# Squares and fourth weight split to GpSimd, factors from the bank, and filler products, in three seams of a two-block transformer kernel

## The chip, the cores and the metric

One Trainium2 chip, one core. The metric is the device time of a whole execution in microseconds, median of several. TensorE multiplies, VectorE, ScalarE and GpSimd work elementwise, SyncE issues most DMAs. Each engine runs its instructions in order; between engines they wait on counting semaphores.

## The reference, cut to what matters

Two transformer blocks over a stream of 512 tokens by 1024 channels, in fp32. The second block is the one touched:

```python
h = x
h = h + 0.5 * rms_norm(swiglu(rms_norm(h, ffn1_pre_g), ...), ffn1_post_g)
u = rms_norm(h, mix_pre_g);  proj = u @ w_in;  ...           # sparse attention, gated recurrence
h = h + rms_norm(merged @ w_out, mix_post_g)
h = h + 0.5 * rms_norm(swiglu(rms_norm(h, ffn2_pre_g), ...), ffn2_post_g)
ple_gate = sigmoid(rms_norm(h, ple_pre_g) @ w_ple_gate)
h = h + rms_norm(ple_gate * (p @ w_ple_proj), ple_post_g)
```

where `rms_norm(x, g) = x * rsqrt(mean(x * x) + eps) * g`.

## The kernel before

The stream lies transposed in SBUF as `x`, eight chunks (k = 0 to 7) of 128 channels by 512 tokens. Weights come as units of 128 by 1024 (or 1408) from HBM into four slots `raw`. To multiply in fp32 with fast passes, every operand is split into a high part (`w_hi`, `a_hi`: a rounded copy, made by ScalarE) and a low part (`w_lo`, `a_lo`: operand minus high part), and each product is three matmuls: hi by hi, lo by hi, hi by lo. `unit_high_part` is ScalarE's half of a weight unit, `split_unit` the other half, on VectorE (L1957, one instruction of 1024 columns) or on GpSimd (L715, four pieces of 256 columns). Units are split in one order, and `unit_split` counts them; a unit's slot is free again when `unit_done` says that TensorE is through with it.

A *seam* is the place where a branch ends, is normed, added to the stream, and the next norm begins. There are three in the second block: behind the first feed-forward (`post1`, then `mixpre` for the stage `proj2`), behind the mixer (`postmix`, then `pre2` for `up3`), and behind the second feed-forward (`post2`, then `plepre` for `ple`). The branch lies kept in `y`. For `post1` and `postmix`, `total_x` on TensorE sums the squares over channels (`sum_columns`, L839, one column of ones) and, when ScalarE has the root and VectorE its inverse, spreads the factor by four transposes over the bank `stat_bank` (`spread`, L872). For `post2` these two lie between products of the small stage `pproj`. Then comes the loop `add_branch` on VectorE, for each chunk k:

- `chunk = y[k] * g[k] * factor` (L2054); the factor is read from the bank for k = 0 and from its copy `rstd` (L1917) afterwards;
- `x[k] += chunk` (L2056);
- the square of chunk k - 1 is added to `sum_sq` (`add_square`: copy L1994, adds L1997), for the next norm;
- `a_lo[k] = x[k] * g'[k] - a_hi[k]` (`scaled_low`, L1963), which waits for ScalarE;
- at some k a weight split: at k = 4 the fourth unit (`first + 3`) of the next stage in the first two seams, at k = 0 and 2 units of `ple` in the third.

ScalarE's side is `scaled_highs` (for `ple` a loop of its own): `a_hi[k] = x[k] * g'[k]` (L1394) when x[k] is there, the square of x[k] into one of two buffers `sq` (L1372), and behind k = 3 the high part of the fourth unit. A square waits until the one two before it is added.

TensorE runs `first_three` (L897 to L899): for each k, as soon as a_lo[k] is there, that chunk's nine matmuls of the stage's first three tiles, since the norm's factor can be applied to the product afterwards. For `mixpre` and `pre2` three more belong to the fourth tile from k = 5 on; for `plepre` the third tile runs two chunks late. Then TensorE sums the squares, does the rest of the fourth tile (L823 to L825) and spreads the factor.

GpSimd does nothing in the seams: ahead of the first it waits for `unit_split` to reach the fourth unit of `proj2`, to split the fifth and later ones; behind its last differences for the recurrence it ends.

Of the kernel before, what the change touches and what calls it, by code (L numbers as in the profile page):

```python
# [38 lines left out]
P = 128  # L39
# [302 lines left out]
def two_blocks(nc, ins, spill, bias_rows, out):  # L342

    with ExitStack() as ctx:
# [362 lines left out]
        def _(pool):  # L707
# [21 lines left out]

            def split_for(t):  # L730

                u = UNIT["proj2"][0] + t + 3
                split_unit(u, BLOCKS_OF[u] * P)
# [18 lines left out]
            pool.wait_ge(unit_split, UNIT["proj2"][0] + SLOTS)  # L752
# [21 lines left out]
            for n in range(HEADS * (NEAR - 1)):  # L774
                make_diff(n)


        @block.tensor
        def _(pe):
# [100 lines left out]
            def total_x(name):  # L880
                sum_x(name)
                spread(name)

# [206 lines left out]
            total_x("post1")  # L1090
# [193 lines left out]
            total_x("postmix")  # L1284
# [44 lines left out]
        def _(act):  # L1329
# [66 lines left out]
            def scaled_highs(stage, g, before, units):  # L1396

                for k in range(DC):
# [3 lines left out]
                    if k == 3:  # L1402
# [491 lines left out]
        def _(dve):  # L1894
# [71 lines left out]
            def scaled_done(stage, units):  # L1966
# [5 lines left out]
                if units.startswith("up"):  # L1972
                    split_unit(UNIT[units][0] + 4)
# [69 lines left out]
            def add_branch(name, g, src, last_read, signal, before, split=None, units={}):  # L2043
# [3 lines left out]
                for k in range(DC + 1):  # L2047
                    if k < DC:
                        if last_read is not None:
                            wait(last_read(k))  # L2050
                        if k >= 2:
                            dve.wait_ge(signal, before + k - 1)
                        factor = rstd if k else stat_bank
                        step(v.scalar_tensor_tensor(chunk[:, k % 2, :], src[:, k, :], prm(g, k), factor[:, :],  # L2054
                                                    ALU.mult, ALU.mult))
                        v.tensor_tensor(x[:, k, :], x[:, k, :], chunk[:, k % 2, :], ALU.add).then_inc(signal, 1)  # L2056
                    if k == 0:
                        take_rstd(name)
                    if k and split:
                        add_square(split[0], k - 1)  # L2060
                    if k < DC and split:
                        scaled_low(split[0], split[1], k)
# [282 lines left out]
            def branch_kept(stage, square_stage):  # L2345
                for k in range(DC):
# [3 lines left out]
                    if k < DC - 1 or square_stage not in LAST_ON_PE:  # L2350
# [6 lines left out]
                       split=("mixpre", "mix_pre_g"), units={4: UNIT["proj2"][0] + 3})  # L2357
# [252 lines left out]
            for m in range(DC):  # L2610
# [13 lines left out]
                if m + 1 < DC:  # L2624
# [6 lines left out]
                       split=("pre2", "ffn2_pre_g"), units={4: UNIT["up3"][0] + 3})  # L2631
            scaled_done("pre2", "up3")
            hiddens("up3", 2)
            for c in range(2):
# [8 lines left out]
                       split=("plepre", "ple_pre_g"), units={0: UNIT["ple"][0] + 1, 2: UNIT["ple"][0] + 2})  # L2643
# [129 lines left out]
```

## Time and profile before

| | us |
|---|---|
| median of 3 runs | 1894.69 |
| lowest and highest | 1892.78, 1895.48 |
| profiled execution | 1894.94 |
| its span, first to last instruction | 1892.8 |

Granted TensorE clock over the span: 0.992 of full speed. Matmuls overlap, so a matmul row shows a longer duration than the distance to the next one. A time in square brackets at the end of a row of the order of time is the idle time of that engine ahead of the instruction, and what ended it.

### The profile page before, as it was taken

How to read it: one execution, taken by the hardware profiler on the slowest of the kernel's cores; microseconds unless marked ns; L12 is line 12 of the kernel's file. 1: busy time of each engine (PE TensorE's matmuls, PEld its weight loads, DVE VectorE, ACT ScalarE, POOL GpSimd, SP SyncE). 2: the span in 40 equal slices, each digit the busy share in tenths (PEclk: the TensorE clock that was granted, in tenths of full speed). 3: DMA queues.
4: the chain of work that ended last, by engine and by line, in shares of the span. 5: the costliest groups of instructions: out<-in, count | busy, mean ns of one | idle time of the engine just before them, and what ended most of it. 6: DMA issues, size and time to landing. Idle time of an engine off the chain costs nothing.

```text
span 1892.8 us, 23659 instructions
## 1 busy us (share of the span) xinstructions
PE 1821.3 (96%) x8356; PEld 1469.0 (78%) x8356; DVE 1089.7 (58%) x1658; ACT 665.9 (35%) x1010; POOL 207.6 (11%) x272
## 2 busy tenths in 40 slices
PE   6998999999999999999989998999898999999988
PEld 4676888888888888888866776789776888888866
DVE  6565588888334655542262677587666655552265
ACT  5333333333223222222243334565453322232244
POOL 2332000000000000000024454433000000000000
PEclk9999999999999999999999999999999999999999
DMA  4677232323222222232222233232341323233211
GB/s 157 61 84 45 89 111 100 100 90 117 94 87 89 89 100 100 90 117 92 83 87 69 95 126 134 73 108 77 117 143 57 102 98 100 92 119 106 83 61 73
DMA packets 55459, 180.61 MB, mean 95 GB/s; under 512 B 6336, under 2 KB 7104, under 8 KB 55392
## 3 DMA queue, kind: packets, MB, share of 16 engines
q1 hardware_dynamic: 43344, 157.33, 24.8%
q10 hardware_dynamic: 12048, 22.40, 7.6%
q8 instruction: 40, 0.66, 0.1%
q14 instruction: 27, 0.22, 0.0%
HBM read 167.65 MB, written 12.06 MB: 95 GB/s over the span
## 4 chain that ended last, share of the span: by engine, by line
PE 82%; DVE 10%; ACT 3%; DMA 2%; issue 2%; ACTq 0%; POOL 0%; SPq 0%; DVEq 0%
PE bank L801 20%; PE bank L802 20%; PE bank L803 20%; PE bank L823 3%; PE bank L825 2%; PE bank L824 2%; DVE score L2399 2%; PE bank L897 2%; PE bank L898 1%; PE bank L899 1%; DVE best L2398 1%; DMA raw<-in_w_proj 1%; PE bank L839 1%; PE bank L1148 1%; PE bank L1232 1%
## 5 line engine op out<-in xcount | busy, mean ns | idle before, releaser
L1341 ACT ACTIVATE w_hi<-raw 128x1024 fp32r<-128x1024 f32 (+2 forms) x281 | 305.0, 1089 | 737.1 <-PE bank L803 625.4
L801 PE MATMUL bank<-a_hi,w_hi 128*128 128x512 f32 x1192 | 467.0, 392 | 3.1 <-DVE gate L2383 2.1
L803 PE MATMUL bank<-a_hi,w_lo 128*128 128x512 f32 x1192 | 464.7, 390 | 0.0
L802 PE MATMUL bank<-a_lo,w_hi 128*128 128x512 f32 x1192 | 464.5, 390 | 0.0
L1957 DVE TENSOR_TENSOR w_lo<-raw,w_hi 128x1024 fp32r<-128x1024 f32 (+2 forms) x222 | 284.2, 1280 | 255.3 <-ACT w_hi L1341 242.0
L801 PEld LDWEIGHTS bank<-a_hi,w_hi 128*128 128x128 f32 x1192 | 224.2, 188 | 57.9 <-issue 7.7
L715 POOL TENSOR_TENSOR w_lo<-raw,w_hi 128x256 fp32r<-128x256 f32 x196 | 150.1, 798 | 1018.0 <-ACT w_hi L1341 1018.0
L803 PEld LDWEIGHTS bank<-a_hi,w_lo 128*128 128x128 f32 x1192 | 224.1, 188 | 47.4
L802 PEld LDWEIGHTS bank<-a_lo,w_hi 128*128 128x128 f32 x1192 | 224.1, 188 | 45.7
L801 PE MATMUL bank<-h_hi,w_hi 128*128 128x512 f32 x528 | 205.4, 389 | 0.0
L802 PE MATMUL bank<-h_lo,w_hi 128*128 128x512 f32 x528 | 205.4, 389 | 0.0
L803 PE MATMUL bank<-h_hi,w_lo 128*128 128x512 f32 x528 | 205.4, 389 | 0.0
L802 PEld LDWEIGHTS bank<-h_lo,w_hi 128*128 128x128 f32 x528 | 99.1, 188 | 20.7
L803 PEld LDWEIGHTS bank<-h_hi,w_lo 128*128 128x128 f32 x528 | 99.1, 188 | 20.6
L801 PEld LDWEIGHTS bank<-h_hi,w_hi 128*128 128x128 f32 x528 | 99.1, 188 | 20.4
L823 PE MATMUL bank<-a_hi,w_hi 128*128 128x512 f32 x250 | 108.0, 432 | 0.0
L825 PE MATMUL bank<-a_hi,w_lo 128*128 128x512 f32 x250 | 99.0, 396 | 0.0
L824 PE MATMUL bank<-a_lo,w_hi 128*128 128x512 f32 x250 | 98.7, 395 | 0.0
L2316 DVE TENSOR_TENSOR val<-bank,rstd 128x512 f32<-128x512 f32 x44 | 30.4, 691 | 113.6 <-PE bank L803 113.6
L897 PE MATMUL bank<-a_hi,w_hi 128*128 128x512 f32 x150 | 63.9, 426 | 31.3 <-DVE a_lo L1963 29.9
L897 PEld LDWEIGHTS bank<-a_hi,w_hi 128*128 128x128 f32 x150 | 29.8, 199 | 45.2 <-DVE a_lo L1963 29.7
L898 PE MATMUL bank<-a_lo,w_hi 128*128 128x512 f32 x150 | 61.2, 408 | 0.0
(330 smaller groups left out, 2315.5 us busy)
## 6 DMA issues: line engine op xcount, KB each, us to landing
raw<-in_w_up SPq DMA_DIRECT2D x132, 512.0 KB, 3.4
raw<-in_w_down SPq DMA_DIRECT2D x48, 704.0 KB, 4.0
raw<-in_w_proj SPq DMA_DIRECT2D x59, 512.0 KB, 3.5
raw<-in_w_wo SPq DMA_DIRECT2D x8, 512.0 KB, 3.6
raw<-in_w_branch SPq DMA_DIRECT2D x16, 256.0 KB, 2.7
gates_in<-spill ACTq DMA_DIRECT2D x16, 256.0 KB, 2.9
raw<-in_w_out SPq DMA_DIRECT2D x8, 512.0 KB, 3.9
raw<-in_w_ple SPq DMA_DIRECT2D x8, 512.0 KB, 3.4
```

The source lines that it names most:

```text
L715: made = pool.tensor_tensor(lo[:, part], src[:, part], hi[:, part].bitcast(F32), ALU.subtract)
L801: mm(dst[:, :], wh, hi[:, k, :], start=(first and c == 0), stop=False)
L802: mm(dst[:, :], wh, lo[:, k, :], start=False, stop=False)
L803: step = mm(dst[:, :], wl, hi[:, k, :], start=False, stop=(last and c == n - 1))
L823: mm(dst[:, :], wh, a_hi[:, c, :], start=(c == 0), stop=False)
L824: mm(dst[:, :], wh, a_lo[:, c, :], start=False, stop=False)
L825: step = mm(dst[:, :], wl, a_hi[:, c, :], start=False, stop=(c == DC - 1))
L897: mm(dst[:, :], wh, hi[:, k, :], start=(k == 0), stop=False)
L898: mm(dst[:, :], wh, lo[:, k, :], start=False, stop=False)
L1341: fn(w_hi[:, slot, 0:size], raw[:, slot, 0:size], ACT.Copy).then_inc(unit_high, 1)
L1957: v.tensor_tensor(w_lo[:, slot, 0:size], raw[:, slot, 0:size], w_hi[:, slot, 0:size].bitcast(F32), ALU.subtract).then_inc(unit_split, 1)
L2399: step(v.match_replace(score[i][:, :], best[:, :], score[i][:, :], TAKEN))
```

## The change

Four edits, all about the three seams.

1. *Squares on GpSimd.* `add_square` leaves the loop of VectorE. GpSimd gets `add_squares`: when the former norm's inverse is there, it copies the first square and adds the other seven, in all three seams. As an operation on GpSimd the add is one instruction of 512 columns.
2. *Fourth split on GpSimd.* For `proj2` and `up3` the fourth unit is split by GpSimd between the squares 2 and 3; ScalarE makes its high part behind k = 2 instead of k = 3. VectorE waits for it ahead of the fifth unit of an `up` stage. In the third seam VectorE keeps its two splits.
3. *Factors from the bank.* The copy to `rstd` is gone, and all eight chunks read the factor from `stat_bank`. The count that frees the bank rises at the last chunk.
4. *Small products.* `total_x` waits for a tile to be read and, behind `spread`, issues twelve products of `ident` and `ones`, 128 by 128 by 128 in plain fp32, into the first auxiliary bank. Nobody reads them. This is in the first two seams.

```diff
+            def add_squares(stage, former, fourth=None):
+
+                pool.wait_ge(inverse_ready, SUM[former] + 1)
+                for k in range(DC):
+                    q = square_at(stage, k)
+                    pool.wait_ge(sq_ready, q + 1)
+                    if k == 0:
+                        pool.tensor_copy(sum_sq[:, :], sq[:, q % 2, :]).then_inc(sum_added, 1)
+                    else:
+                        pool.wait_ge(sum_added, q)
+                        pool.tensor_tensor(sum_sq[:, :], sum_sq[:, :], sq[:, q % 2, :], ALU.add).then_inc(sum_added, 1)
+                    if fourth and k == 2:
+                        pool.wait_ge(unit_split, UNIT[fourth][0] + 3)
+                        split_unit(UNIT[fourth][0] + 3, DC * P)
+
...
             split_units("wo", 0, SLOTS)
-            pool.wait_ge(unit_split, UNIT["proj2"][0] + SLOTS)
+            add_squares("mixpre", "post1", "proj2")
             split_units("proj2", SLOTS, LEAD2 + 3)
...
                 make_diff(n)
+            add_squares("pre2", "postmix", "up3")
+            add_squares("plepre", "post2")
...
-            def total_x(name):
+            def total_x(name, idle):
+
+                wait(tile_read(idle, 0))
                 sum_x(name)
                 spread(name)
+                for _ in range(12):
+                    mm(bank[BANKS][:, 0:P], ident[:, :], ones[:, :], start=True, stop=True)
...
-            total_x("post1")
+            total_x("post1", "up2")
...
-            total_x("postmix")
+            total_x("postmix", "out")
...
-                    if k == 3:
+                    if k == 2:
                         unit_high_part(UNIT[units][0] + 3)
...
                 if units.startswith("up"):
+                    dve.wait_ge(unit_split, UNIT[units][0] + SLOTS)
                     split_unit(UNIT[units][0] + 4)
...
-            def add_branch(name, g, src, last_read, signal, before, split=None, units={}):
+            def add_branch(name, g, src, last_read, signal, before, split, units={}):
 
                 invert(name)
                 dve.wait_ge(spread_ready, STAT[name] + 1)
-                for k in range(DC + 1):
-                    if k < DC:
-                        if last_read is not None:
-                            wait(last_read(k))
-                        if k >= 2:
-                            dve.wait_ge(signal, before + k - 1)
-                        factor = rstd if k else stat_bank
-                        step(v.scalar_tensor_tensor(chunk[:, k % 2, :], src[:, k, :], prm(g, k), factor[:, :],
-                                                    ALU.mult, ALU.mult))
-                        v.tensor_tensor(x[:, k, :], x[:, k, :], chunk[:, k % 2, :], ALU.add).then_inc(signal, 1)
-                    if k == 0:
-                        take_rstd(name)
-                    if k and split:
-                        add_square(split[0], k - 1)
-                    if k < DC and split:
-                        scaled_low(split[0], split[1], k)
+                for k in range(DC):
+                    wait(last_read(k))
+                    if k >= 2:
+                        dve.wait_ge(signal, before + k - 1)
+                    step(v.scalar_tensor_tensor(chunk[:, k % 2, :], src[:, k, :], prm(g, k), stat_bank[:, :],
+                                                ALU.mult, ALU.mult))
+                    if k == DC - 1:
+                        dve.sem_inc(rstd_ready, 1)
+                    v.tensor_tensor(x[:, k, :], x[:, k, :], chunk[:, k % 2, :], ALU.add).then_inc(signal, 1)
+                    scaled_low(split[0], split[1], k)
                     if k in units:
                         split_unit(units[k])
...
-                       split=("mixpre", "mix_pre_g"), units={4: UNIT["proj2"][0] + 3})
+                       ("mixpre", "mix_pre_g"))
...
-                       split=("pre2", "ffn2_pre_g"), units={4: UNIT["up3"][0] + 3})
+                       ("pre2", "ffn2_pre_g"))
...
-                       split=("plepre", "ple_pre_g"), units={0: UNIT["ple"][0] + 1, 2: UNIT["ple"][0] + 2})
+                       ("plepre", "ple_pre_g"), units={0: UNIT["ple"][0] + 1, 2: UNIT["ple"][0] + 2})
```

## Rows read from the trace of the kernel before

**Rows 1.** The page's chain that ended last, shares by engine.

```profile
PE 82%; DVE 10%; ACT 3%; DMA 2%; issue 2%; ACTq 0%; POOL 0%; SPq 0%; DVEq 0%
```

**Rows 2.** Stretches: length, busy by engine (x instructions), granted clock, DMA share, GB/s.

```profile
947.70:976.20 28.50, 22.17 (x90) 16.63 (x89) 23.22 (x34) 10.92 (x17) 0.00 (x0) 0.89 0.17 53
1436.50:1465.10 28.60, 22.98 (x91) 17.74 (x90) 23.23 (x34) 10.92 (x17) 0.00 (x0) 0.88 0.06 19
1813.40:1845.10 31.70, 24.57 (x104) 18.04 (x102) 25.49 (x36) 14.06 (x23) 0.00 (x0) 1.00 0.17 54
...
951.20:954.40 3.20, 3.20 (x8) 2.59 (x9) 2.71 (x5) 1.24 (x2) 0.00 (x0) 0.55 0.17 67
```

**Rows 3.** VectorE in order of time, first seam: start, duration, instruction [idle before].

```profile
950.08 0.75 DVE L1963 SCALAR_TENSOR_TENSOR a_lo<-x,par,a_hi 128x512 fp32r<-128x512 f32 x1 [0.26 <-ACT a_hi L1394]
...
957.40 0.69 DVE L2056 TENSOR_TENSOR x<-x,chunk 128x512 f32<-128x512 f32 x1
...
958.01 0.69 DVE L1997 TENSOR_TENSOR sum_sq<-sum_sq,sq 128x512 f32<-128x512 f32 x1
...
958.88 0.75 DVE L1963 SCALAR_TENSOR_TENSOR a_lo<-x,par,a_hi 128x512 fp32r<-128x512 f32 x1 [0.19 <-ACT a_hi L1394]
...
960.33 0.69 DVE L2056 TENSOR_TENSOR x<-x,chunk 128x512 f32<-128x512 f32 x1
...
962.49 1.22 DVE L1957 TENSOR_TENSOR w_lo<-raw,w_hi 128x1024 fp32r<-128x1024 f32 x1
...
963.62 0.75 DVE L2054 SCALAR_TENSOR_TENSOR chunk<-y,par,rstd 128x512 f32<-128x512 f32 x1
```

**Rows 4.** ScalarE in order of time, first seam.

```profile
949.26 0.72 ACT L1394 ACTIVATE a_hi<-x,par 128x512 fp32r<-128x512 f32 x1 [2.73 <-DVE x L2056]
...
958.12 0.73 ACT L1394 ACTIVATE a_hi<-x,par 128x512 fp32r<-128x512 f32 x1 [1.69 <-DVE x L2056]
...
958.75 0.61 ACT L1372 ACTIVATE sq<-x 128x512 f32<-128x512 f32 x1
```

**Rows 5.** TensorE in order of time: its waits for a_lo, first and second seam.

```profile
951.20 0.77 PE L897 MATMUL bank<-a_hi,w_hi 128*128 128x512 f32 x1 [3.49 <-DVE a_lo L1963]
...
959.69 0.50 PE L897 MATMUL bank<-a_hi,w_hi 128*128 128x512 f32 x1 [0.57 <-DVE a_lo L1963]
...
1451.48 0.50 PE L897 MATMUL bank<-a_hi,w_hi 128*128 128x512 f32 x1 [0.41 <-DVE a_lo L1963]
```

**Rows 6.** GpSimd and VectorE side by side, in the first block's projections.

```profile
38.15 1.18 POOL L715 TENSOR_TENSOR w_lo<-raw,w_hi 128x256 fp32r<-128x256 f32 x1
...
38.77 1.10 DVE L2134 TENSOR_TENSOR q<-unrot,cos 128x512 f32<-128x512 f32 x1
...
107.88 0.69 DVE L2138 TENSOR_TENSOR silu<-bank,sin 128x512 f32<-128x512 f32 x1 [1.99 <-PE bank L981]
...
107.89 1.42 POOL L715 TENSOR_TENSOR w_lo<-raw,w_hi 128x256 fp32r<-128x256 f32 x2
...
108.61 1.25 DVE L2141 TENSOR_TENSOR k<-k,silu 128x512 f32<-128x512 f32 x1
```

**Rows 7.** GpSimd undisturbed: one unit's four pieces; one add of 512 columns.

```profile
978.89 2.81 POOL L715 TENSOR_TENSOR w_lo<-raw,w_hi 128x256 fp32r<-128x256 f32 x4 [799.13 <-ACT w_hi L1341]
...
1183.73 1.27 POOL L768 TENSOR_TENSOR diagonal<-t_bias,score 128x512 f32<-128x512 f32 x1 [1.61 <-DVE logit L2489]
```

**Rows 8.** TensorE, plain fp32 products of 128 columns, two records each.

```profile
1242.94 1.16 PE L1215 MATMUL bank<-hq,hk 128*128 128x128 f32 x8
```

**Rows 9.** Third seam: ScalarE's high part that waits for a DMA, and a_lo(2).

```profile
1822.50 1.06 ACT L1341 ACTIVATE w_hi<-raw 128x1024 fp32r<-128x1024 f32 x1 [1.37 <-DMA raw<-in_w_ple]
...
1824.21 0.75 DVE L1963 SCALAR_TENSOR_TENSOR a_lo<-x,par,a_hi 128x512 fp32r<-128x512 f32 x1 [1.30 <-ACT a_hi L1394]
```

**Rows 10.** End of the first seam: the sum on TensorE, the fifth unit's high part.

```profile
975.42 0.95 PE L839 MATMUL bank<-ones,sum_sq 128*128 128x1 f32 x8
...
977.75 1.06 ACT L1341 ACTIVATE w_hi<-raw 128x1024 fp32r<-128x1024 f32 x1 [1.08 <-DMA raw<-in_w_proj]
```

## The prediction

> **What bounds the kernel now.** I read the page first, then the busy time of each engine in the stretches that the change touches, then the order of time on VectorE, ScalarE and TensorE inside one of them. The chain that ended last lies 82% on TensorE [rows 1]. The change touches no part of that: it works in three seams, where a branch is added to the stream and the next norm is prepared. There TensorE is busy 22 to 25 us of 28.5, 28.6 and 31.7 us, VectorE 23 to 25, GpSimd not at all [rows 2]. So a seam has its own limit, and it is read one step k at a time.
>
> One step of the first seam, from the start of `x += chunk` (L2056) at 957.40 to the next at 960.33, is 2.93 us [rows 3]. The reader should see what stands between. x ends at 958.09; ScalarE starts a_hi at 958.12, and VectorE's a_lo starts at 958.88, as a_hi ends [rows 3, 4]. The sum of squares (L1997) lies at 958.01 to 958.69, inside that wait for ScalarE. The path is x, a_hi, a_lo, the next chunk, the next x; the square's sum is not on it. TensorE waits for a_lo at k = 3 (959.69) and, in the second seam, at k = 4 (1451.48): it has caught up there, whatever the first products cost [rows 5].
>
> **Squares taken off VectorE.** Seven adds of 0.69 us and a copy leave VectorE in each seam, but they filled a gap that stays: gain 0. The last add stood behind a_lo(7), while TensorE still had 12 products to do; it reached the sum only at 975.42 [rows 10]. Also 0.
>
> **Factors read from the bank.** The copy into `rstd` at k = 0 goes. a_lo(0) started 0.82 us after a_hi(0) (950.08 behind 949.26), in the later steps 0.76 us [rows 3, 4]: gain 0.07 us in the first and second seam.
>
> **The fourth split on GpSimd.** In the first seam VectorE's split starts at 962.49 and the next chunk at 963.62, so 1.13 us leave the path; the same in the second. In the third the splits at k = 0 and 2 stay. By itself the change would give 2 x (1.13 + 0.07) = 2.4 us. ScalarE's high part moves from k = 3 to k = 2 and takes 1.06 us inside an idle stretch of 1.69 us before the next a_hi [rows 4, 10]: 0. The wait that is added ahead of VectorE's fifth split, and the one ahead of the seam's add on GpSimd, come long after their events: 0. What is queued behind the squares on GpSimd is the split of the fifth unit, whose high part waits for its DMA until 977.75 [rows 10]; the last add would end about 1.5 us after its square, some 2 us before TensorE reaches the sum. 0.
>
> **What GpSimd's work does to VectorE.** This is the term that decides. In the seams GpSimd was silent; the trace has it beside VectorE elsewhere. GpSimd's pieces run to 109.31, VectorE's add with two SBUF inputs starts at 108.61 and takes 1.25 us instead of 0.69: it ends at 109.86, 0.55 behind the piece. Again: a piece ends at 39.33, VectorE's `q` at 39.87, 0.54 behind. A VectorE product whose one input lies in PSUM takes 0.69 us beside a running piece [rows 6]. The other way round, a piece that is behind a VectorE instruction takes 1.18 instead of 0.70 us. So the two take turns, whole instructions at a time, when VectorE reads two SBUF tensors. In the loop these are x += chunk and a_lo; the chunk itself now reads y and the bank, one SBUF tensor.
>
> The Trainium skill has this as a rule (SBUF — State Buffer, Who interferes with whom): a VectorE instruction with two SBUF inputs contends with a GpSimd instruction that reads SBUF, and whoever is first holds the interface for its whole instruction. It speaks against this change. The trace agrees for pieces of 256 columns, as just read; no row shows it for a GpSimd add of 512 columns. With the rule carried over to such an add the sum is a loss of 3.8 us; were it not to hold there, the gain of 2.4 us would stand.
>
> Now one step with it, from the start of x at 0. The square runs from 1.35 to 1.96 [rows 3, 4]. GpSimd starts 0.08 later (its usual lag behind ScalarE: 977.75 + 1.06 to 978.89 [rows 7, 10]). a_lo holds the inputs until 2.23. An add of 512 columns alone takes 1.27 us [rows 7], of which I take 0.14 to lie ahead of the reading, as on VectorE (0.69 alone, 0.55 behind a piece), so GpSimd ends at 2.23 + 1.13 = 3.36. The next x wants to start at 2.93 and would end at 3.62; it ends at 3.36 + 0.55 = 3.91. **0.29 us are lost in each step.** The bounds: 0, if the add gives way in between; 0.55, if GpSimd starts its add 0.3 us later (2.34 + 1.27 + 0.55 = 4.16). I take 0.29, since the two pairs of [rows 6] agree to 0.01 us. The copy at k = 0 has no row; a copy reads one tensor, and the time that it may take before it costs anything is about 1.0 us from its start. I take 0; at an add's length it would cost 0.29 in the first two seams.
>
> First and second seam, instruction by instruction under that rule: x(2) 0.29, x(3) 0.28, then the four pieces of the split (2.81 us alone [rows 7]) start: a_lo(3) waits 0.32 for the second, x(4) 0.45 for the fourth, a_lo(4) 0.16 for the add of square 3, which queued behind the split; x(5), x(6), x(7) 0.29, 0.30, 0.30. Sum 2.39, less 1.20: **+1.19 us in each.** Third seam: a_lo(2) waits 1.30 us for ScalarE, which had waited for a weight's DMA (its w_hi starts at 1822.50) [rows 9], so what x(2) loses is hidden. x(3) to x(7) lose 5 x 0.29 = **1.45 us**, and nothing is given back, since no split leaves VectorE there. TensorE works straight on behind a_lo(7) in all three, and the loads it releases move with it, so these sums reach the end.
>
> **Twelve small products.** Not shown in the trace are ident-by-ones products. Four products of 128 columns are 8 records in 1.16 us with a last tail, 0.25 us each [rows 8]; twelve make 3.0 us. They start behind the transposes, at about 947.5, in a wait of 3.49 us that ends at 951.20 [rows 5]. They end about 0.3 us before a_lo(0) does. Would they overrun by 1 us, the steps k = 1 and 2 hide it: 9 products at 0.24 us are 2.2 of 2.93 us. They keep the granted clock up (0.89 and 0.88 in the first two seams, 1.00 in the third [rows 2]); in the first products it was at its lower level, 1.2 of 2.4 GHz, for most of the time: 8 products took 3.20 us at a mean of 0.55, 0.40 us each, where the third seam has 104 in 24.57 us, 0.24 each [rows 2]. But TensorE had caught up by k = 3, so this is 0 on the path.
>
> **Sum.** 2 x 1.19 + 1.45 = 3.8 us. The profiled execution took 1894.94 us (span 1892.8, 2.1 around it) and becomes 1898.8; it lies 0.25 over the median of the runs, 1894.69, so the forecast for the median is **1898.5 us**. A measurement of this kernel can tell about 0.2% (3.8 us) from no change; the forecast stands on that line.
>
> **Rivals.** (1) *No meeting*: GpSimd's add gives way inside its instruction, VectorE loses nothing, and the split's 1.13 us count: 1894.7 - 2.4 = 1892.3. Over the 17 steps that meet an add, the kernel is quicker only while a step loses under 0.14 us (2.4 / 17). Against it are the rows of 256 columns; for it, only that no 512-column add met such an instruction. 8%. (2) *Half a meeting*: the add holds only for the length of a 256 piece at a time, so x waits for nothing and only the split's pieces cost some 0.6 us a seam: 1894.7 - 2 x 0.6 = 1893.5; with a loss of 0.1 to 0.2 per step 1895 to 1897. Together 17%. (3) *A worse meeting*: the square's sum starts 0.3 us later, by GpSimd's waits or a longer copy, and then each x loses 0.55: 17 x 0.26 = 4.4 more, 1902.9; half of that gives 1900.7. It decides from a lag of some 0.15 us behind the square, where a_lo no longer hides the start. For it: two waits stand ahead of each add. Against it: a lag of 0.08 us. 15%. (4) *The clock on the path*: were the slow products of the first steps what TensorE's end hangs on, keeping the clock up would give 9 x 0.16 = 1.4 us in each of the first two seams: 1898.5 - 2.9 = 1895.6. Against it are TensorE's waits for a_lo at k = 3 and 4. The Trainium skill (TensorE: Matmul & The Clock Gate, What's actually happening) says that an idle TensorE falls to 1.2 GHz and that work releases it; the clock of the first seam agrees (0.89), but the rule says nothing of who waits. 2%. (5) *The products overrun* their wait or the whole change costs nothing it can show: 1894 to 1895, in (2).
>
> **How the numbers follow.** Forecast 58%, with its own range 1897.0 to 1900.0, split by the 0.2% line at 1898.5 about in half, a little more above it since the copy and the waits can only add. Slower by over 0.2%: 0.33 of the forecast, and the 15% of (3): 0.48. Faster by over 0.2% would be under 1890.9, which (1) does not reach by itself; with (4) it could: 0.03, for all that isn't thought of too. The rest is within: 0.49. The range leaves out (1), the lower part of (2) and the upper part of (3): 1894.5 to 1902.0.
>
> **What would show it.** In the profile after: x += chunk and a_lo at 0.69 and 0.75 us alone, x about 1.0 us in the steps 2 to 7 of each seam; steps 3.2 us apart instead of 2.93; GpSimd's adds about 1.3 us, starting 0.1 us behind each square; the four pieces of the split partly 1.1 us long; the seams 1.2, 1.2 and 1.5 us longer from the first chunk to the sum on TensorE; clock 1.00 in the first two. If x stays at 0.69 us, (1) is right and the kernel is quicker. If TensorE runs without a gap between k = 3 and 7, (4) is. The prediction is wrong, too, if a copy on GpSimd takes much over 1 us, or if seams behind these move.

## The result and the profile after

| | us |
|---|---|
| changed kernel, median of 11 runs | 1899.27 (1896.50 to 1899.88) |
| kernel before, median of 11 runs beside it | 1894.59 (1890.78 to 1898.52) |
| ratio of the two, 95% interval | 1.0025 [1.0017, 1.0033] |
| profiled execution of the changed kernel, its span | 1899.80, 1898.0 |

The changed kernel is slower by 0.25%, 4.7 us (3.2 to 6.3 by the interval). The forecast was 1898.5 us for the median, 3.8 us more than before; the median is 1899.27, inside its range of 1897.0 to 1900.0. It has new line numbers: x += chunk is L2077, the chunk L2073, a_lo L1984, a_hi L1415, the square L1393, GpSimd's copy L737 and add L740.

In this document a seam's length is read from VectorE's order of time, from the start of the first x += chunk to the end of the last a_lo:

| seam, us | 1 | 2 | 3 | sum |
|---|---|---|---|---|
| before | 23.98 | 23.98 | 26.59 | 74.55 |
| after | 25.18 | 25.19 | 28.20 | 78.57 |
| more | 1.20 | 1.21 | 1.61 | 4.02 |
| predicted | 1.19 | 1.19 | 1.45 | 3.83 |

Now the page. Its chain by engine, which answers [rows 1], and the costs of the first line and of the groups that are new or moved (x is the count, mean in ns behind the busy time):

```profile
PE 1830.9 (96%) x8404; PEld 1478.1 (78%) x8404; DVE 1077.6 (57%) x1629; ACT 665.6 (35%) x1010; POOL 245.7 (13%) x304
...
PE 81%; DVE 10%; DMA 3%; ACT 3%; issue 2%; ACTq 0%; POOL 0%; SPq 0%; DVEq 0%
...
L737 POOL COPY sum_sq<-sq 128x512 f32<-128x512 f32 x3 | 2.2, 733 | 1253.3 <-ACT sq L1393 1253.3
```

Read alone, these lines mislead twice. The chain gives GpSimd 0% although its adds are what the kernel lost time to: an instruction that is held up is shown as a longer instruction, not as a wait, so the time stands under VectorE's name. And VectorE has less work than before, while the kernel is longer.

The stretches of the three seams, to set beside [rows 2] (length, busy by engine with x instructions, granted clock, DMA share, GB/s; they begin and end with the seams of this kernel):

```profile
948.00:976.20 28.20, 23.67 (x103) 18.30 (x102) 19.24 (x24) 10.90 (x17) 14.12 (x12) 0.94 0.13 41
1438.90:1467.60 28.70, 24.15 (x106) 18.70 (x105) 19.25 (x24) 10.90 (x17) 14.13 (x12) 0.94 0.02 3
1816.90:1850.10 33.20, 25.86 (x103) 18.99 (x101) 23.58 (x27) 14.07 (x23) 10.93 (x8) 0.95 0.15 50
```

VectorE works 19.2 us in 24 instructions where it had 23.2 in 34; GpSimd works 14.1 where it had none. The loop got slower all the same. One step shows why. VectorE in order of time in the first seam:

```profile
953.90 0.74 DVE L2073 SCALAR_TENSOR_TENSOR chunk<-y,par,bank 128x512 f32<-128x512 f32 x1
954.68 1.00 DVE L2077 TENSOR_TENSOR x<-x,chunk 128x512 f32<-128x512 f32 x1
956.48 0.75 DVE L1984 SCALAR_TENSOR_TENSOR a_lo<-x,par,a_hi 128x512 fp32r<-128x512 f32 x1 [0.79 <-ACT a_hi L1415]
957.14 0.74 DVE L2073 SCALAR_TENSOR_TENSOR chunk<-y,par,bank 128x512 f32<-128x512 f32 x1
957.92 1.01 DVE L2077 TENSOR_TENSOR x<-x,chunk 128x512 f32<-128x512 f32 x1
```

ScalarE and GpSimd in the same step:

```profile
955.72 0.72 ACT L1415 ACTIVATE a_hi<-x,par 128x512 fp32r<-128x512 f32 x1 [2.00 <-DVE x L2077]
956.35 0.61 ACT L1393 ACTIVATE sq<-x 128x512 f32<-128x512 f32 x1
```

```profile
953.80 1.33 POOL L740 TENSOR_TENSOR sum_sq<-sum_sq,sq 128x512 f32<-128x512 f32 x1 [2.25 <-ACT sq L1393]
957.04 1.34 POOL L740 TENSOR_TENSOR sum_sq<-sum_sq,sq 128x512 f32<-128x512 f32 x1 [1.91 <-ACT sq L1393]
```

GpSimd's add runs from 953.80 to 955.13. x += chunk starts under it at 954.68 and ends at 955.68, 0.55 behind the add, as it ended 0.55 behind a piece in [rows 6]. The chunk, which starts during the add as well, takes its usual 0.74: of its inputs only y lies in SBUF. The next x starts at 957.92, 3.24 us on, against 2.93 in [rows 3].

### The profile page after: what moved, and what is told of

The parts are those of the page before. It is cut to its first block, busy times and chain, and to the rows that moved or that the text cites. A ratio compares the mean times of both kernels' runs of the same rounds, so it can differ in the third digit from the quotient of the medians.

```text
span 1898.0 us, 23765 instructions
## 1 busy us (share of the span) xinstructions
PE 1830.9 (96%) x8404; PEld 1478.1 (78%) x8404; DVE 1077.6 (57%) x1629; ACT 665.6 (35%) x1010; POOL 245.7 (13%) x304
## 4 chain that ended last, share of the span: by engine, by line
PE 81%; DVE 10%; DMA 3%; ACT 3%; issue 2%; ACTq 0%; POOL 0%; SPq 0%; DVEq 0%
PE bank L818 20%; PE bank L819 20%; PE bank L820 20%; PE bank L840 2%; PE bank L842 2%; PE bank L841 2%; DMA raw<-in_w_proj 2%; DVE score L2415 2%; DVE best L2414 1%; PE bank L918 1%; PE bank L919 1%; PE bank L920 1%; DVE x L2077 1%; PE bank L856 1%; PE bank L1169 1%
## 5 line engine op out<-in xcount | busy, mean ns | idle before, releaser
L819 PE MATMUL bank<-a_lo,w_hi 128*128 128x512 f32 x1192 | 464.6, 390 | 0.0
L715 POOL TENSOR_TENSOR w_lo<-raw,w_hi 128x256 fp32r<-128x256 f32 x204 | 156.5, 799 | 225.5 <-ACT w_hi L1362 225.5
L737 POOL COPY sum_sq<-sq 128x512 f32<-128x512 f32 x3 | 2.2, 733 | 1253.3 <-ACT sq L1393 1253.3
L841 PE MATMUL bank<-a_lo,w_hi 128*128 128x512 f32 x250 | 99.5, 398 | 0.0
```

Of the source, the lines that this page charges most:

```text
L715: made = pool.tensor_tensor(lo[:, part], src[:, part], hi[:, part].bitcast(F32), ALU.subtract)
L819: mm(dst[:, :], wh, lo[:, k, :], start=False, stop=False)
L841: mm(dst[:, :], wh, a_lo[:, c, :], start=False, stop=False)
```

## The experiments

In the table the first seam stands for the first two, which agree to 0.1 us in each kernel but where the text says otherwise. "Ratio" is to the kernel before, run beside it.

| kernel | seam 1 | seam 3 | step | median, us | ratio, 95% interval |
|---|---|---|---|---|---|
| before | 23.98 | 26.59 | 2.93 | see below | |
| after | 25.18 | 28.20 | 3.24 | 1899.27 | 1.0025 [1.0017, 1.0033] |
| squares only | 30.54 | 31.91 | 3.95 | 1913.23 | 1.0096 [1.0080, 1.0113] |
| squares and bank | 26.50 | 28.12 | 3.24 | 1901.33 | 1.0036 [1.0024, 1.0048] |
| split only | 24.47 | 26.58 | 2.93 | 1893.95 | 1.0006 [0.9996, 1.0015] |
| after, adds left out | 23.60 | 27.36 | 2.93 | 1893.68 | 0.9999 [0.9989, 1.0008] |
| after, adds in quarters | 24.89 | 28.16 | 3.25 | 1897.47 | 1.0017 [1.0008, 1.0027] |
| small products only | 23.97 | 26.54 | 2.93 | 1894.54 | 1.0000 [0.9990, 1.0009] |
| chunk ahead | 20.40 | 24.13 | 2.53 | 1885.63 | 0.9953 [0.9940, 0.9967] |
| chunk ahead, small products | 20.40 | 24.18 | 2.53 | 1884.49 | 0.9951 [0.9937, 0.9964] |
| after, chunk ahead | 24.83 | 28.07 | 3.24 | 1897.61 | 1.0019 [1.0009, 1.0029] |

Medians of different rows should be compared by their ratios, since the kernel before was run anew beside each group. The median of the kernel before was 1894.59 beside the changed one; 1893.27 beside the squares only, the split only, the adds left out and the adds in quarters; 1894.44 beside the last row and 1894.04 beside the other four.

**Squares on GpSimd alone.** The factor is still copied to `rstd`, the split stays on VectorE, there are no small products.

```diff
+            add_squares("mixpre", "post1")
...
+            add_squares("pre2", "postmix")
+            add_squares("plepre", "post2")
...
-                    if k and split:
-                        add_square(split[0], k - 1)
```

> The kernel before with one edit: the sums of squares of the three seams go to GpSimd; split, factor copy and TensorE's order stay. Theory (VectorE and GpSimd take turns at SBUF, whole instructions at a time): each x += chunk from k = 2 on ends 0.55 us behind GpSimd's add and takes 1.0 us instead of 0.69, steps 3.24 us apart; behind VectorE's own split at k = 4 GpSimd's add comes later and the next x loses about 1 us. Seams 1 and 2 longer by 2.5 us each, seam 3 by 1.6: 6.6 us, 1901.2. Rival 1 (the loss comes from the split or the small products, the adds cost nothing): x at 0.69 us, seams as before, 1894.6. Rival 2 (the small products or the clock made the rest of the difference): seams as by the rival it goes with.

Measured: 1.0096 [1.0080, 1.0113], four times the loss of the whole change, and the seams 30.54, 30.52 and 31.91 us, 18.4 us more than before in sum. A clear miss: I had not counted the chunk. VectorE, then GpSimd, one step:

```profile
953.52 1.78 DVE L2069 SCALAR_TENSOR_TENSOR chunk<-y,par,rstd 128x512 f32<-128x512 f32 x1
955.34 0.69 DVE L2071 TENSOR_TENSOR x<-x,chunk 128x512 f32<-128x512 f32 x1
956.82 0.75 DVE L1978 SCALAR_TENSOR_TENSOR a_lo<-x,par,a_hi 128x512 fp32r<-128x512 f32 x1 [0.79 <-ACT a_hi L1409]
```

```profile
953.42 1.34 POOL L740 TENSOR_TENSOR sum_sq<-sum_sq,sq 128x512 f32<-128x512 f32 x1 [2.63 <-ACT sq L1387]
```

With the factor in `rstd` the chunk reads two SBUF tensors, y and `rstd`. It comes 0.10 us behind the start of GpSimd's add, waits for all of it, and takes 1.78 us instead of 0.74. x is then free, at 0.69. So a step loses 1.02 us.

**Squares and the bank factor.** The same with all chunks reading the bank.

```diff
-                        factor = rstd if k else stat_bank
-                        step(v.scalar_tensor_tensor(chunk[:, k % 2, :], src[:, k, :], prm(g, k), factor[:, :],
+                    step(v.scalar_tensor_tensor(chunk[:, k % 2, :], src[:, k, :], prm(g, k), stat_bank[:, :],
...
-                    if k == 0:
-                        take_rstd(name)
```

> The kernel before with two edits: sums of squares on GpSimd, and all eight chunks with their factor from the bank. With the squares alone, chunk = y * g * rstd read two SBUF tensors, came 0.1 us behind the start of GpSimd's add, and each step took 3.95 us. Theory (what counts is two SBUF inputs): with the factor in PSUM the chunk no longer waits; the next x does, 0.31 us a step, and about 1 us once behind VectorE's split at k = 4: steps 3.24 us, seams 1 and 2 at 26.5 us from the first x to the end of a_lo(7) (23.98 before, 30.5 with the squares alone), seam 3 at 28.2. 6.6 us over the kernel before. Rival (the copy into rstd or its wait made the steps long, or GpSimd slows VectorE whatever it reads): steps still 3.9 us.

Measured: as expected, steps of 3.24 and seams of 26.50, 26.50 and 28.12. Reading the factor from the bank is worth 30.54 - 26.50 = 4.0 us in each of the first two seams and 3.8 in the third, once GpSimd adds the squares, where the copy that it saves is worth some 0.07. VectorE around its split, in this kernel:

```profile
961.07 2.31 DVE L1972 TENSOR_TENSOR w_lo<-raw,w_hi 128x1024 fp32r<-128x1024 f32 x1
963.30 0.73 DVE L2066 SCALAR_TENSOR_TENSOR chunk<-y,par,bank 128x512 f32<-128x512 f32 x1
```

The split, started 0.10 us behind an add at 960.97, takes 2.31 us instead of the 1.22 of [rows 3].

**The fourth split alone.** Squares and factor as before; GpSimd splits the fourth unit.

```diff
+            pool.wait_ge(unit_split, UNIT["proj2"][0] + 3)
+            split_units("proj2", 3, SLOTS)
...
+            pool.wait_ge(unit_split, UNIT["up3"][0] + 3)
+            split_units("up3", 3, SLOTS)
...
-                    if k == 3:
+                    if k == 2:
...
+                    dve.wait_ge(unit_split, UNIT[units][0] + SLOTS)
...
-                       split=("mixpre", "mix_pre_g"), units={4: UNIT["proj2"][0] + 3})
+                       split=("mixpre", "mix_pre_g"))
```

> The kernel before with one edit: the fourth split of proj2 and up3 is made by GpSimd, its high part behind k = 2; the squares stay on VectorE. Theory: 1.13 us of VectorE's split leave the path, but GpSimd's four pieces meet x, the square's add and a_lo of one and a half steps, all with two SBUF inputs, and give nearly all of it back: seams 1 and 2 the same within 0.3 us each, seam 3 unchanged, 1894.7. Rival (only adds of 512 columns hurt, pieces of 256 slip between): 1.13 us less in each of two seams, 1892.3.

Measured: 1.0006 [0.9996, 1.0015], first two seams 0.49 us longer (expected: the same within 0.3), the third unchanged: no gain, and the sign in the seams is a loss. VectorE under the four pieces, and the pieces:

```profile
956.15 1.23 DVE L2001 TENSOR_TENSOR sum_sq<-sum_sq,sq 128x512 f32<-128x512 f32 x1
957.30 1.22 DVE L1966 SCALAR_TENSOR_TENSOR a_lo<-x,par,a_hi 128x512 fp32r<-128x512 f32 x1
958.45 1.22 DVE L2058 SCALAR_TENSOR_TENSOR chunk<-y,par,rstd 128x512 f32<-128x512 f32 x1
959.70 1.11 DVE L2060 TENSOR_TENSOR x<-x,chunk 128x512 f32<-128x512 f32 x1
```

```profile
955.68 4.58 POOL L715 TENSOR_TENSOR w_lo<-raw,w_hi 128x256 fp32r<-128x256 f32 x4 [777.43 <-ACT w_hi L1344]
```

Four VectorE instructions in a row meet a piece each, since here all four read two SBUF tensors; they lose 0.54, 0.47, 0.47 and 0.42. About 0.3 of the first lies in the wait for ScalarE; the rest is 1.6 us, more than the 1.13 that the split gave back. The four pieces take 4.58 us instead of 2.81 [rows 7].

**The change without the adds.** The seven adds of each seam are left out, so that the norm's sum is that of the first square alone; the copy stays and the counts are kept.

```diff
-                        pool.tensor_tensor(sum_sq[:, :], sum_sq[:, :], sq[:, q % 2, :], ALU.add).then_inc(sum_added, 1)
+                        pool.sem_inc(sum_added, 1)
```

> The changed kernel with GpSimd's seven adds of each seam left out (the norm's sum is then that of the first square alone); all waits and counts stay. Theory: x += chunk back to 0.69 us but for the steps beside the split. Against the changed kernel seams 1 and 2 shorter by 1.6 us each and seam 3 by 1.6: 4.8 us, so 1894.5 and about 1 us below the kernel before inside the first two seams together. Rival (the loss sits in the added waits, the place of the split or the small products): no more than 0.5 us change in a seam, 1899.

Measured: the first two seams 1.58 and 1.61 us shorter than in the changed kernel, as expected; the third only 0.84, because its a_lo(2) came 0.58 late behind the weight's DMA. From the start of x(3) to the end of a_lo(7) it takes 14.06 us, against 15.48: 1.42 less. The steps are 2.93 again, and x and chunk have their old lengths but for those under the split's pieces:

```profile
958.04 0.69 DVE L2077 TENSOR_TENSOR x<-x,chunk 128x512 f32<-128x512 f32 x1
959.52 1.05 DVE L1984 SCALAR_TENSOR_TENSOR a_lo<-x,par,a_hi 128x512 fp32r<-128x512 f32 x1 [0.79 <-ACT a_hi L1415]
960.50 0.73 DVE L2073 SCALAR_TENSOR_TENSOR chunk<-y,par,bank 128x512 f32<-128x512 f32 x1
961.27 1.15 DVE L2077 TENSOR_TENSOR x<-x,chunk 128x512 f32<-128x512 f32 x1
```

So the adds are the whole loss of the change. Without them it is level with the kernel before, 0.9999 [0.9989, 1.0008], and not quicker, for two reasons that the seams show. In the first two the pieces take back 0.30 + 0.46 of the split's 1.13, so that they are only 0.38 and 0.40 shorter than before. The third is 0.77 longer than before, and 0.68 of that is the weight's later landing (its w_hi starts 9.01 us behind x(0) instead of 8.33).

**The adds in quarters.** If the loss comes from whole instructions taking turns, shorter ones should cost less.

```diff
-                        pool.tensor_tensor(sum_sq[:, :], sum_sq[:, :], sq[:, q % 2, :], ALU.add).then_inc(sum_added, 1)
+                        for at in range(0, T, P):
+                            part = slice(at, at + P)
+                            made = pool.tensor_tensor(sum_sq[:, part], sum_sq[:, part], sq[:, q % 2, part], ALU.add)
+                        made.then_inc(sum_added, 1)
```

> The changed kernel with each GpSimd add of 512 columns made as four of 128. Theory of turns by whole instructions: x waits at most for the rest of one quarter, a few tenths at most, though GpSimd is busy longer in sum (about 1.7 us a square): seams 1 and 2 shorter than in the changed kernel by 0.7 us each, seam 3 by about 1: 2.4 us, 1896.9. Rival (it is the amount of data that GpSimd reads, not the length of its instruction): no shorter, or longer by 0.1 to 0.4 us a step, 1899 to 1905.

Measured: 0.29, 0.61 and 0.04 us shorter than the changed kernel, largely a miss. VectorE, then GpSimd, in one step:

```profile
955.43 1.01 DVE L2080 TENSOR_TENSOR x<-x,chunk 128x512 f32<-128x512 f32 x1
```

```profile
954.55 2.21 POOL L742 TENSOR_TENSOR sum_sq<-sum_sq,sq 128x128 f32<-128x128 f32 x4 [1.03 <-ACT sq L1396]
```

Here x still takes 1.01 us. In the first seam x(2) and x(3) lose as much as with whole adds. The second quarter's end, the third's start (5.86 us behind x(0)) and the start of x(2) (5.85) fall together; the third quarter goes first and ends at 6.32, where the whole add would have ended at 6.30, and x ends 0.55 behind it. In the second seam the same two starts fall the other way: x(2) takes 0.69 and the quarter 1.00 instead of 0.46. One step later, at 1444.08, x takes 1.01 again. So the turns are taken between quarters too, but at x(2) hundredths of a microsecond decide who goes first. The 0.29 of the first seam come from elsewhere: a_lo(3) and a_lo(4) take 0.77 us each, where they took 1.04 and 0.90 beside whole adds. GpSimd's work gets longer by the cut (2.21 us for 1.33): behind the split it runs twelve quarters without a pause (7.03 us), and the step from x(5) to x(6) grows from 3.24 to 3.41. Whether another cut would pay stays open.

**The small products alone.**

```diff
+                wait(tile_read(idle, 0))
...
+                for _ in range(12):
+                    mm(bank[BANKS][:, 0:P], ident[:, :], ones[:, :], start=True, stop=True)
```

> The kernel before with one edit: the twelve small products behind the spread in the first two seams. Theory (TensorE waits for a_lo again by k = 3 or 4, so its first products are off the path): granted clock in the first stretch of the two seams higher than before, from the first x += chunk to the end of a_lo(7) 23.98 us in both as before, time within 1 us of the kernel before. Rival (the slow first products are on the path): 1.4 us less in each of two seams, 1891.

Measured: 1.0000 [0.9990, 1.0009]; the seams 23.97, 23.96 and 26.54; from x(0) to the sum on TensorE 26.91 us, before 26.89. As expected, off the path.

**A rival order of the loop: the next chunk made ahead.** If the path of the kernel before is x, a_hi, a_lo, chunk, x, as the prediction had it, then the chunk can be made while ScalarE makes a_hi. The kernel before, with the bank factor and this order; squares and splits stay on VectorE:

```diff
+                make_chunk(0)
+                for k in range(DC):
+                    dve.wait_ge(dve_step, steps[0])
...
                     v.tensor_tensor(x[:, k, :], x[:, k, :], chunk[:, k % 2, :], ALU.add).then_inc(signal, 1)
+                    if k + 1 < DC:
+                        make_chunk(k + 1)
```

> The kernel before, squares and split left on VectorE, factor from the bank, and chunk k + 1 made between x += chunk of k and a_lo of k instead of behind it. Theory (a step is a round trip x, a_hi on ScalarE, a_lo, chunk, and its 0.79 us wait for ScalarE can hold useful work): the chunk fills the wait and a step is the sum of VectorE's four instructions, 2.65 us instead of 2.93. a_lo(7) of seams 1 and 2 2.0 to 2.3 us earlier, of which TensorE (12 products, 2.86 us a step from k = 5) lets 1.0 to 1.5 through; seam 3 1.1 to 1.4 us. 3.5 to 4.3 us off the kernel before, 1890. Rival (VectorE's busy time is the limit as it is, the order does not matter): steps 2.9 us, time as before.

Measured: 0.9953 [0.9940, 0.9967], 8.4 us quicker than the kernel before by the medians and, by the two ratios, 13.6 quicker than the changed one. That is about twice what I had given it: I had let 1.0 to 1.5 us of each of the first two seams through to TensorE's sum, and 2.8 came through. VectorE, one step:

```profile
950.80 0.69 DVE L2060 TENSOR_TENSOR x<-x,chunk 128x512 f32<-128x512 f32 x1
951.40 0.74 DVE L2052 SCALAR_TENSOR_TENSOR chunk<-y,par,bank 128x512 f32<-128x512 f32 x1
952.06 0.68 DVE L1997 TENSOR_TENSOR sum_sq<-sum_sq,sq 128x512 f32<-128x512 f32 x1
952.66 0.75 DVE L1963 SCALAR_TENSOR_TENSOR a_lo<-x,par,a_hi 128x512 fp32r<-128x512 f32 x1
953.33 0.69 DVE L2060 TENSOR_TENSOR x<-x,chunk 128x512 f32<-128x512 f32 x1
```

VectorE has no idle time left in the step, which is 2.53 us, the sum of its four instructions (0.60 + 0.66 + 0.60 + 0.67, start to start). The seams are 3.6 us shorter; the sum on TensorE comes 24.12 us behind x(0) instead of 26.89, only 2.8 sooner, since TensorE now ends last there (3.7 us behind the end of a_lo(7), before 2.9). 2 x 2.8 + 2.5 in the third seam are 8.1 of the 8.4.

**The same with the small products.** If TensorE is the limit now, its clock may count.

> The kernel of chunk_ahead with the twelve small products in seams 1 and 2. With shorter steps TensorE is nearly the limit, so its slow first products may now leave a backlog that reaches k = 5. Theory: up to 1 us less in each of the two seams than chunk_ahead, from the first x to the sum on TensorE; 0.5 to 2 us less in all, 1889. Rival (still hidden): the same as chunk_ahead within 0.3 us a seam.

Measured: 0.9951 [0.9937, 0.9964], from x(0) to the sum 24.08 us against 24.12. The small products are worth nothing that can be measured here either.

**The change with the next chunk made ahead.** The same order in the changed kernel, that is without squares on VectorE.

> The changed kernel with chunk k + 1 made between x += chunk of k and a_lo of k. On the kernel before this brought a step from 2.93 to 2.53 us. Theory of turns: here it brings next to nothing. VectorE comes back to x half a microsecond earlier and waits that much longer for GpSimd's add, which starts behind the square and ends at the same distance from the last x; a step stays at 3.2 us, seams 1 and 2 at 24.9 us (25.2 in the changed kernel), seam 3 at 28.2, 1899. Rival (the add's cost is a fixed 0.3 us a step, whatever the order): steps 2.53 + 0.31 = 2.84 us, seams 1 and 2 at 22.5 us, seam 3 near 26, 1892.

Measured: 1.0019 [1.0009, 1.0029], seams 24.83, 24.80 and 28.07: 0.35 less than the changed kernel in the first two and 4.4 more than the chunk made ahead in the kernel before. The step is 3.24 again. VectorE, GpSimd, ScalarE:

```profile
953.73 1.78 DVE L2082 TENSOR_TENSOR x<-x,chunk 128x512 f32<-128x512 f32 x1
955.43 0.73 DVE L2074 SCALAR_TENSOR_TENSOR chunk<-y,par,bank 128x512 f32<-128x512 f32 x1
956.30 0.75 DVE L1984 SCALAR_TENSOR_TENSOR a_lo<-x,par,a_hi 128x512 fp32r<-128x512 f32 x1
956.97 1.78 DVE L2082 TENSOR_TENSOR x<-x,chunk 128x512 f32<-128x512 f32 x1
```

```profile
953.62 1.33 POOL L740 TENSOR_TENSOR sum_sq<-sum_sq,sq 128x512 f32<-128x512 f32 x1 [1.90 <-ACT sq L1393]
956.86 1.33 POOL L740 TENSOR_TENSOR sum_sq<-sum_sq,sq 128x512 f32<-128x512 f32 x1 [1.91 <-ACT sq L1393]
```

```profile
955.54 0.72 ACT L1415 ACTIVATE a_hi<-x,par 128x512 fp32r<-128x512 f32 x1 [2.00 <-DVE x L2082]
956.17 0.61 ACT L1393 ACTIVATE sq<-x 128x512 f32<-128x512 f32 x1
```

This is the most telling of the runs. VectorE is ready for x at 953.73, and the add has begun 0.11 us earlier; x waits for all of it and ends 0.56 behind it. Then a_hi, the square, and the next add starts at 956.86. Both kernels have the same circle: add 1.33, x 0.55 behind it, 1.36 from the end of x over a_hi and the square to the next add, 3.24 in all. What the chunk does is no longer in it. So GpSimd's add is not a disturbance beside the path, it has become a link of it.

**The kernel before once more,** one execution.

> The kernel before, unchanged, for a second profile of it. Theory: the seams are the same to 0.05 us (23.98, 23.98, 26.6 us), while the start of the kernel and the stretch between the first and the second seam differ by up to 2 us from one execution to the next with the granted clock, so 1.2 us of the 5.2 us between the two profiled executions are not the change's. Rival: those stretches repeat to 0.1 us too, and the change did cost 1.2 us outside its seams.

Measured: 1894.14 us; seams 23.97, 23.95 and 26.57, which agree with the first profile to 0.03 us. The stretch between the first and the second seam differs by 0.3 us and the start of the first seam by 0.4, so the swing of up to 2 us that I expected there does not show in these two. So the differences of the seams above are far beyond what two executions differ by.

## Why the prediction was right

**The path of a step** held. x, a_hi, a_lo, chunk: the chunk made ahead took 0.40 us off each step, and the squares' leaving took nothing off (2.93 without the adds, as before). So the adds filled a gap that stays, and their gain is 0, as forecast.

**The meeting with GpSimd's add** held in kind and size: x took 1.00 us where I had 0.98, the step 3.24 where I had 3.22. Leaving out the adds took 1.6 us off each of the first two seams and all of the loss. Rivals 1 and 2, no meeting or half a one, fell with the same rows; rival 3, a worse one, fell with the add's start 0.08 us behind the end of the square (956.35 + 0.61 to 957.04). Two qualifications. I called the 0.29 a loss that comes on top of the old path; it is what is left when a new, closed path of 3.24 us takes over, which the chunk made ahead did not shorten (3.24 in both orders). And the size came from ends that agree to 0.01 us in [rows 6], not from the mechanism behind them: the 0.55 us from GpSimd's end to VectorE's is measured again in each of these kernels.

The Trainium skill (SBUF — State Buffer, Who interferes with whom) gives two rules that these runs bear out. One is the line between one and two SBUF inputs: with the factor in `rstd` the chunk took 1.78 us beside an add, with the factor in the bank 0.74. The other is that the order of issue decides who waits: a start 0.10 us behind the other engine's costs the whole of its instruction.

**The step by step of the first seam:** x(2) 0.31 (predicted 0.29), x(3) 0.31 (0.28), a_lo(3) 0.29 (0.32), x(4) 0.45 (0.45), a_lo(4) 0.15 (0.16), x(5) to x(7) 0.31, 0.31 and 0.33 (0.89 together). Sum 2.46 (2.39), less 1.14 for the split and 0.08 at x(1). That makes 1.24, and start to start the steps add up to the 1.20 of the table; a duration is read to a hundredth, so the eight items are no better than that. The last of the eight, x(7), has a part of its own: it is held 0.12 us by the count that now rises between chunk and x, an instruction that I had put at nothing; it comes as late in the kernel without the adds, so the add has no part in that. Coming later, it loses only 0.21 to the add (it takes 0.90). GpSimd around the split, whose four pieces held a_lo(3) and x(4) and whose queue pushed the add of square 3 into a_lo(4):

```profile
957.04 1.34 POOL L740 TENSOR_TENSOR sum_sq<-sum_sq,sq 128x512 f32<-128x512 f32 x1 [1.91 <-ACT sq L1393]
958.34 3.71 POOL L715 TENSOR_TENSOR w_lo<-raw,w_hi 128x256 fp32r<-128x256 f32 x4
962.00 1.73 POOL L740 TENSOR_TENSOR sum_sq<-sum_sq,sq 128x512 f32<-128x512 f32 x1
```

**The split** was right in the sum and wrong in a sentence. I wrote that by itself the change would give 2.4 us. The split alone gave nothing: 0.49 us more in a seam. In the changed kernel it is a gain (26.50 to 25.18), for there it takes VectorE's long split out of the way of an add that made it 2.31 us long, and the chunk is immune.

**The bank factor** was the undersized term, in meaning though not in the sum. I put it at 0.07 us and noted only in passing that the chunk now reads one SBUF tensor. That note is worth 4.0 us a seam: the squares alone stand at 1.0096, with the bank factor at 1.0036. The whole change without the bank factor was not run. Here the prediction was right by a line that it read rightly and did not price.

**The copy** had no row, and I took 0 under 1.0 us. It took 0.61 in the first two seams and x(1) 0.69: 0, as taken. In the third it took 0.98, for there a split of VectorE (1820.24 to 1821.46) was under way when it began at 1820.95; this cost nothing either.

**The third seam** lost 1.61 for 1.45: x(3) to x(7) lost 1.5 in place of 5 x 0.29, and 0.1 comes from ScalarE and the DMA around a_lo(2), less what the bank factor gave. x(2) was held for 0.76 (it took 1.45, from 1825.08) and the wait behind it hid that, as the prediction had it.

**The small products and the clock.** Their worth, nothing, was right, and so it is alone and with the chunk ahead. The profile of them that I forecast was wrong. I had them last 3.0 us, end 0.3 us before a_lo(0) does, and keep the granted clock at 1.00. TensorE in order of time, and the clock in two stretches:

```profile
947.81 4.47 PE L903 MATMUL bank<-ones,ident 128*128 128x128 f32 x24
952.04 0.47 PE L918 MATMUL bank<-a_hi,w_hi 128*128 128x512 f32 x1
```

```profile
947.80:951.20 3.40, 3.40 (x18) 3.40 (x17) 2.33 (x4) 1.24 (x2) 0.26 (x1) 0.50 0.88 263
951.20:954.60 3.40, 3.40 (x21) 2.95 (x20) 2.57 (x4) 1.25 (x2) 1.15 (x2) 1.00 0.18 67
```

The clock fell to its lower level (0.50, that is 1.2 GHz) as they began, and stayed there for 3.4 of their 4.5 us. So the first weight product starts at 952.04, 1.0 us behind the end of a_lo(0) (951.06); in the kernel before it started at 951.20, 0.4 us behind. The full clock came earlier than there (1.00 from 951.2 on, where [rows 2] has 0.55) and TensorE waited for a_lo again from k = 2 on. Both differences are swallowed by that wait. In the third seam the first profile of before has the full clock throughout, the changed kernel 0.51 between 1828.4 and 1831.8. The change did not bring this about by its longer steps: the second profile of before has 0.50 from 1825.4 to 1831.4, and the kernel with squares and bank, whose steps are 3.24 too, has 1.00 for all of its third seam. TensorE waits for a_lo again behind such a stretch, and the seam is as long with it (26.57) as without it (26.59). So rival 4, the clock on the path, fell, and the overrun of rival 5 came, by 1.0 us, and was hidden in the first two seams as the prediction had said that it would be.

**What is left over.** The profiled execution took 4.9 us more than that of before, 5.2 in the span; the seams hold 4.0. Of the rest 0.3 lies ahead of the first seam and 0.85 between the first and the second. There the largest piece is at the start of the sparse attention, where TensorE waits 3.3 us in both kernels and then runs at the lower clock for longer after the change. The stretches, first of after, then of before:

```profile
1156.00:1162.80 6.80, 5.74 (x15) 4.05 (x16) 4.14 (x11) 2.82 (x9) 3.52 (x5) 0.50 0.00 0
```

```profile
1155.40:1158.80 3.40, 2.65 (x6) 1.83 (x7) 2.34 (x7) 1.97 (x7) 2.48 (x3) 0.51 0.00 0
1158.80:1162.20 3.40, 3.40 (x19) 2.69 (x18) 2.41 (x7) 1.45 (x4) 1.42 (x2) 0.99 0.00 0
```

I don't charge this to the change. The work between the seams is the same in all these kernels. Its length was 464.87 and 464.57 us in the two profiles of before and 465.72 after. In the other nine it lay between 463.38 (chunk ahead with small products) and 466.85 (squares and bank). The change with the chunk ahead, which holds every edit of the change, had 464.39. With 3.5 us between the ends it comes and goes by more than the 0.85 in question, but the ends belong to kernels that differ, and the two profiles of one kernel differ by 0.3 only. That the change has no part in it is argued from this spread, not shown. The forecast, 3.8 us, is to be held against the seams' 4.0; for the 0.7 by which the whole kernel's 4.7 goes beyond them no cause is shown. Both the seams' 4.0 us and the span's 5.2 lie within the 3.2 to 6.3 of the timed runs.

## What to carry to other kernels

Before work is moved to GpSimd, count for each VectorE instruction that it will run beside how many SBUF tensors it reads: those with one kept their usual length here, those with two wait for the whole of a GpSimd instruction that began a moment sooner, and if that instruction depends on VectorE's own result, the two close into a circle that sets the step. Take work off an engine only if it lies on the path: the squares filled a gap, and filling the same gap with the next chunk instead was worth 8 us where the change that moved them cost 5. Edits of one loop don't add up: the split's move was a loss alone and a gain beside the squares, and the bank factor's worth was 0.07 or 4 us.

## What the runs showed of the hardware

- A GpSimd copy of 128 by 512 fp32 took 0.61 us, an add of the same size 1.33: twice for the second input. The Trainium skill (GPSIMD Engine Reference, Engine selection) says that GpSimd takes about twice VectorE's time with two inputs and runs at roughly line rate with one. VectorE's add took 0.69, so the trace agrees on the first. On the second, VectorE's own copy took 0.42 in the loop with the chunk ahead, so GpSimd's took about one and a half times as long.
- A VectorE instruction of 512 columns with two SBUF inputs that met a GpSimd instruction ended 0.55 us behind it, were it a piece of 256 columns, a whole add or a quarter of one. Started 0.10 us behind an add, it took 1.78 us; a split of 1024 columns 2.31.
- In the chain that ended last such a hold shows nowhere: GpSimd stands at 0%. It is to be seen only as a row whose duration is longer than the same row elsewhere, with a GpSimd row over its start.
- Twelve plain fp32 products of 128 columns that ran right behind a wait ran at the lower clock themselves for 3.4 of their 4.5 us (0.50); the clock was at 1.00 when the products that matter came. Their worth was nothing, with TensorE waiting (1.0000) and with TensorE ending last (0.9951 beside 0.9953).
